# Routed experts of a two-block transformer layer: w3's products with both row halves as one stationary, and seven places for split weight pieces

## The reference, cut to what matters

```python
def first_block(...):
    ...
    ret = head_groupnorm(retention_chunkwise(qh, kh, vh)).reshape(B, S, RET_V_DIM)
    y_a = (ret * jax.nn.silu(z_ret)) @ w_ret_out[l]
    a = u_val * jax.nn.sigmoid(u_gate)
    a = causal_depthwise_conv(a, conv_w[l], conv_b[l])
    a = jax.nn.silu(layernorm(a, conv_ln_g[l], conv_ln_b[l]))
    y_b = (a * jax.nn.silu(z_conv)) @ w_conv_out[l]
    ...
def hierarchical_moe(h, w_router_group, w_router_expert, w1, w3, w2):
    ...
    def run_block(args):
        xblk, e = args
        hid = jax.nn.silu(xblk @ w1[e]) * (xblk @ w3[e])
        return hid @ w2[e]
    ...
```

## Time and profile before

| | |
|---|---|
| median of 3 runs | 1822.02 us |
| profiled execution: its own time | 1816.51 us |
| profiled execution: span from first to last instruction | 1814.7 us |
| mean granted TensorE clock | 0.966 of full |
| busy: TensorE, DVE, ACT, POOL | 93%, 62%, 50%, 47% of the span |
| transfers | 340.94 MB, mean 188 GB/s |

### The profile page before, as it was taken

How to read it: one execution, slowest core, us unless ns; L and a number is a source line. 1 busy time by engine, 2 the same in 40 slices (tenths; PEclk the granted TensorE clock), 3 DMA queues, 4 the chain that set the end, 5 groups by cost and what they waited for, 6 DMA issues and landing times.

```text
span 1814.7 us, 23104 instructions
## 1 busy us (share of the span) xinstructions
PE 1688.7 (93%) x7444; PEld 1240.8 (68%) x7444; DVE 1127.6 (62%) x1455; ACT 914.0 (50%) x1228; POOL 861.7 (47%) x451
## 2 busy tenths in 40 slices
PE   2899999989999999899899997967999999999996
PEld 2788888677878787778656786764565666656654
DVE  5776773562232575435354454256999899998996
ACT  4544542532223332243242234334888888888885
POOL 0688886233434244334002331203766777667774
PEclk9899999999999999999899998988999999999998
DMA  8344353222122062613111511055999999999994
GB/s 301 106 112 122 115 193 104 99 93 99 62 84 93 20 242 98 232 47 135 47 69 71 160 53 41 0 232 203 359 376 371 378 374 373 383 372 390 383 375 149
DMA packets 135406, 340.94 MB, mean 188 GB/s; under 512 B 14581, under 2 KB 66045, under 8 KB 110506
## 3 DMA queue, kind: packets, MB, share of 16 engines
q1 hardware_dynamic: 127938, 320.71, 48.7%
q0 software_dynamic: 5200, 8.41, 2.1%
q10 hardware_dynamic: 2200, 10.92, 1.5%
HBM read 329.78 MB, written 18.87 MB: 192 GB/s over the span
## 4 chain that ended last, share of the span: by engine, by line
PE 65%; POOL 10%; issue 9%; DVE 8%; ACT 4%; DMA 2%; DVEq 1%; POOLq 0%; ACTq 0%; SPq 0%
PE ps L710 16%; PE ps L711 16%; PE ps L712 16%; POOL parts L2363 7%; PE ps L682 5%; PE ps L914 3%; PE ps L1058 3%; PE ps L692 2%; POOL out L2386 2%; PE ps L1059 2%; ACT arena L1481 2%; DVE arena L2254 1%; DMA ring<-in_w_ada 1%; PE ps L903 1%; PE ps L1020 1%
## 5 line engine op out<-in xcount | busy, mean ns | idle before, releaser
L2330 POOL TENSOR_TENSOR parts<-ring,parts 128x1024 fp32r<-128x1024 f32 x158 | 392.2, 2488 | 705.7 <-ACT parts L1108 656.3
L710 PE MATMUL ps<-parts,act_parts 128*128 128x512 f32 (+2 forms) x1152 | 453.6, 394 | 13.7 <-DVEq L1738 5.3
L712 PE MATMUL ps<-parts,act_parts 128*128 128x512 f32 (+2 forms) x1152 | 449.1, 390 | 0.0
L711 PE MATMUL ps<-parts,act_parts 128*128 128x512 f32 (+2 forms) x1152 | 448.6, 389 | 0.0
L1451 ACT CAST parts<-ring 128x1024 fp32r<-128x1024 f32 x384 | 396.4, 1048 | 93.5 <-PE ps L712 70.0
L2214 DVE TENSOR_TENSOR parts<-ring,parts 128x1024 fp32r<-128x1024 f32 x289 | 394.4, 1415 | 25.1 <-ACT parts L1451 18.2
L1108 ACT CAST parts<-ring 128x1024 fp32r<-128x1024 f32 x158 | 163.9, 1048 | 348.7 <-PE ps L712 305.2
L2363 POOL TENSOR_TENSOR parts<-ring,parts 128x1024 fp32r<-128x1024 f32 x95 | 262.3, 2761 | 143.7 <-ACT parts L1451 143.0
L710 PEld LDWEIGHTS ps<-parts,act_parts 128*128 128x128 f32 (+1 forms) x1152 | 190.0, 165 | 105.5 <-POOL parts L2363 18.8
L710 PE MATMUL ps<-act_parts,parts 128*128 128x512 f32 x640 | 252.2, 394 | 5.2 <-DVEq L1641 5.2
L711 PE MATMUL ps<-act_parts,parts 128*128 128x512 f32 x640 | 249.9, 390 | 0.0
(11 more groups left out here) (265 smaller groups left out, 1794.6 us busy)
## 6 DMA issues: line engine op xcount, KB each, us to landing
ring<-in_w SPq DMA_DIRECT2D x192, 1024.0 KB, 7.4
ring<-in_w_in SPq DMA_DIRECT2D x30, 1024.0 KB, 7.3
ring<-in_w_in SPq DMA_DIRECT2D x34, 512.0 KB, 5.2
ring<-in_w_ada SPq DMA_DIRECT2D x12, 1024.0 KB, 15.0
ring<-in_w_ret_out SPq DMA_DIRECT2D x8, 1024.0 KB, 6.2
ring<-in_w_out SPq DMA_DIRECT2D x8, 1024.0 KB, 8.6
ring<-in_w_in SPq DMA_DIRECT2D x16, 256.0 KB, 4.1
gates_dram<-arena ACTq DMA_DIRECT2D x8, 512.0 KB, 5.8
```

Source lines behind the costliest of these rows:

```text
L710: pe.matmul(o, lhs[1], rhs[0], start=start, stop=False)
L711: pe.matmul(o, lhs[0], rhs[1], start=False, stop=False)
L712: return pe.matmul(o, lhs[0], rhs[0], start=False, stop=stop)
L2330: pool.tensor_tensor(parts[:, g % 4, 1, :], ring[:, st.place(j), k * 1024:(k + 1) * 1024], parts[:, g % 4, 0, :].bitcast(F32), ALU.subtrac ...
```

## The change

In the experts:

- The parts get seven places: piece n of a block stands in place n % 7, four of them in `parts` and three in a stretch of `act_parts` that is free at that time. TensorE frees them by two semaphores, `up_used` and `down_used`.
- w3's products take both halves of the rows as one stationary of 128x128, as w2's did: two matmuls for each 128 rows of the weight in place of three. `xgT` is laid out for it.
- The result of w3 then has low rows; ACT copies them (`low_up`, L1481 of the changed kernel, a copy of 64x512) and DVE adds them (`up_sum`, L2273) before `hidden`'s product (L2279), whose operands are then all in SBUF.
- The gate is one step: ACT's Silu of w1's product; DVE's `gate` is gone.

In the first block Silu takes the place of a sigmoid and a product in the same way, for z (L1254, L1745 are gone) and for the convolution (L1230, L1232, L1728 become one Silu).

The diff, cut to its core. The places:

```diff
+        more_parts = act_parts[:, 2048:8192].rearrange("p (s h n) -> p s h n", s=3, h=2)
+        def piece_parts(n):
+            return parts[:, n % 7] if n % 7 < 4 else more_parts[:, n % 7 - 4]
```

TensorE, `up`:

```diff
-                for j in range(2):
-                    o = bank(stage, 1 + j, i)[0:SLOTS, :]
-                    for n in range(4):
-                        pe.wait_ge(piece_split[4 * j + n], b + 1)
-                        for c in range(2):
-                            t = 2 * n + c
-                            mm = split_product(o, hi_lo(xgT[:, :, t, :]), hi_lo(parts[:, n, :, c * 512:(c + 1) * 512]),
...
+                for n in range(8):
+                    if n % 4 == 0:
+                        o = bank(stage, 1 + n // 4, i)
+                    pe.wait_ge(piece_split[n], b + 1)
+                    w = piece_parts(n)
+                    for c in range(2):
+                        t = 2 * (n % 4) + c
+                        half = slice(c * 512, (c + 1) * 512)
+                        if n < 4:
+                            mm = split_product(o[0:SLOTS, :], [xgT[:, t, h, :] for h in range(2)], [w[:, h, half] for h in range(2)],
                                                t == 0, t == KT - 1)
                         else:
+                            rows = xgT[:, t].rearrange("p h s -> p (h s)")
+                            pe.matmul(o, rows, w[:, 0, half], start=t == 0, stop=False)
+                            mm = pe.matmul(o, rows, w[:, 1, half], start=False, stop=t == KT - 1)
```

ACT, in the convolution and in the experts:

```diff
-                    own(act.activation(convT[:, t, :], convT[:, t, :], ACT.Identity, bias=bias, scale=g))
-                    own.wait()
-                    act.activation(ln_s[:, t % 2, :], convT[:, t, :], ACT.Sigmoid).then_inc(ln_s_ready, 1)
+                    act.activation(convT[:, t, :], convT[:, t, :], ACT.Silu, bias=bias, scale=g).then_inc(ln_s_ready, 1)
...
+            def gate(stage, i=0):
+                drained(stage, 1, act.activation(t_h[0:SLOTS, :], full(stage, 1, i)[0:SLOTS, :], ACT.Silu))
+            def low_up(stage, i=0):
+                act.copy(up_low[0:SLOTS, :], full(stage, 2, i)[SLOTS:2 * SLOTS, :]).then_inc(up_low_ready, 1)
...
+            def round(b, i):
+                high(7, b, used=(up_used, b * 6 + 1))
+                gate("moe", i)
+                for n in (8, 9):
+                    high(n, i, used=(up_used, b * 6 + (n - 6)))
+                high(10, i)
+                high(11, i, used=(up_used, b * 6 + 4))
+                low_up("moe", i)
+                high_rows("moe", 0, i)
...
             with act.Fori(0, act.snap(steps - 1)) as r:
-                up("moe", r + 2, 0, r + 1, ends=("moe", 5, r))
+                high(0, r + 2, ends=("moe", 2, r))
+                for n in (1, 2, 3):
+                    high(n, r + 2, used=(down_used, r * 3 + n))
                 low_rows(r)
                 high_hidden("moe", r)
-                up("moe", r + 2, 4, r + 1, ends=("moe", 1, r + 1))
-                down(r + 1)
-                high_rows("moe", 0, r + 1)
+                for n in (4, 5, 6):
+                    high(n, r + 2)
+                round(r + 2, r + 1)
```

DVE, in the convolution and in the experts:

```diff
-                        own(dve.tensor_tensor(convT[:, q, :], convT[:, q, :], ln_s[:, q % 2, :], ALU.mult))
-                        own.wait()
...
+            def hidden(stage, b, i=0):
+                dve.wait_ge(up_low_ready, b + 1)
+                moe(dve.tensor_tensor(up_sum[0:SLOTS, :], full(stage, 2, i)[0:SLOTS, :], up_low[0:SLOTS, :], ALU.add))
                 moe.wait()
+                drained(stage, 2, dve.nop())
...
-                moe(dve.scalar_tensor_tensor(out=hid[0:SLOTS, :], in0=full(stage, 2, i)[0:SLOTS, :], scalar=w,
+                moe(dve.scalar_tensor_tensor(out=hid[0:SLOTS, :], in0=up_sum[0:SLOTS, :], scalar=w,
                                              in1=t_h[0:SLOTS, :], op0=ALU.mult, op1=ALU.mult))
...
                 for n in (4, 5, 6):
                     low(n, r * 12 + (20 + n))
-                gate("moe", r + 2, r + 1)
                 for n in (8, 9, 10):
                     low(n, r * 12 + (20 + n))
```

More of the change, by code:

```diff
@@ L386, in build @@
         y_low = carve([D])
+        up_low, up_sum = carve([FF]), carve([FF])
         block_w = block_oh
@@ L452, in build @@
         piece_used = [sem(f"parts{n}_used") for n in range(4)]
-        moe_used = [sem(f"moe_parts{n}_used") for n in range(3)]
+        up_used, down_used, up_low_ready = sem("up_pieces_used"), sem("down_pieces_used"), sem("up_low_rows_ready")
         dense_split = sem("dense_pieces_split")
@@ L1250, in _ @@
                 for m in range(MT):
-                    o = full(f"hz{h}", m)
-                    if m >= 2:
-                        act.wait_ge(sig_r_used, h * MT + (m - 1))
-                    act.activation(sig_r[:, m % 2, :], o, ACT.Sigmoid).then_inc(sig_r_ready, 1)
+                    own(act.activation(z_tok[:, m, :], full(f"hz{h}", m), ACT.Silu))
+                    own.wait()
+                    drained(f"hz{h}", m, act.nop())
+                    act.nop().then_inc(z_ready, 1)
                 ahead(g + 12)
@@ L1468, in high_rows @@
             def high_rows(stage, k, i=0):
-                act.copy(xgT[:, 0].rearrange("p t n -> p (t n)"), full(stage, k, i)).then_inc(xgT_hi, 1)
-            def up(stage, b, first, i=0, ends=None):
-                for n in range(first, first + 3):
-                    high(n, b, used=pieces[stage].before(n, i))
-                high(first + 3, b, ends=ends)
-                if first == 4:
-                    act.activation(sg_h[0:SLOTS, :], full(stage, 1, i)[0:SLOTS, :], ACT.Sigmoid).then_inc(sg_h_ready, 1)
+                act.copy(xgT[:, :, 0, :], full(stage, k, i).rearrange("p (t n) -> p t n", t=KT)).then_inc(xgT_hi, 1)
+            def gate(stage, i=0):
+                drained(stage, 1, act.activation(t_h[0:SLOTS, :], full(stage, 1, i)[0:SLOTS, :], ACT.Silu))
+            def low_up(stage, i=0):
+                act.copy(up_low[0:SLOTS, :], full(stage, 2, i)[SLOTS:2 * SLOTS, :]).then_inc(up_low_ready, 1)
             def low_rows(c):
@@ L1740, in head_rows @@
             def head_rows(h):
-                for m in range(MT):
-                    o = full(f"hz{h}", m)
-                    dve.wait_ge(sig_r_ready, h * MT + m + 1)
-                    own(dve.tensor_tensor(z_tok[:, m, :], o, sig_r[:, m % 2, :], ALU.mult))
-                    own.wait()
-                    dve.nop().then_inc(sig_r_used, 1)
-                    drained(f"hz{h}", m, dve.nop())
                 dve.wait_ge(decay_in, (h + 1) * 16)
@@ L2292, in _ @@
                 low(n, 8 + n)
-            gate("moe", 1)
             for n in (8, 9, 10):
```

94 lines of the change are left out of this document (42 added, 52 removed).

## The result

| | before | after |
|---|---|---|
| median of 4 runs each | 1821.88 us | 1937.22 us (1934.97 to 1940.58) |
| ratio | | 1.0635, 95% interval 1.0619 to 1.0651 |
| profiled execution: its own time, span | 1816.51, 1814.7 us | 1940.58, 1938.7 us |
| a round, mean of 29 (first to thirtieth scatter) | 17.36 us | 21.68 us |

The change makes the kernel 6.3% slower. The 29 rounds grew by 29 x 4.32 = 125.3 us and the whole span by 124.0 us, so the rest of the program, the first block's gain included, comes out at about zero in these two profiles.

A forecast was written before the change was run, and what follows sets the result against it. With the change, DVE's queue, held up by POOL's lows, was to bound the rounds: 15.06 + 6.60 - 0.4 = 21.3 us. Rounds +118 us and first block -8.5 us gave 1926, forecast as a 1931 us median, range 1840 to 1965 us.

The forecast's parts named there:

- TensorE is not alone at its end: Experts' rounds: w3's fewer matmuls save TensorE 1.8 us a round, worth its price only if TensorE is last.
- A block costs 2.20 us, and there are three in a round: Experts' rounds: three POOL lows each hold up a DVE instruction with two SBUF inputs, 2.20 us each, 6.60 us together.
- The prediction's other price: Experts' rounds: POOL's whole shortest low, 2.34 us, per block instead of 2.20; 0.4 us more a round, some 13 us in all.
- Where they fall: DVE's round: POOL's low 7 blocks low 8, low 11 blocks low 9, low 3 blocks the next round's low 0.
- the sign of two long lows between low 6 and the product: DVE's round: two DVE lows in a row at 3.3 us or more there would show the forecast right.
- Low 11 without a wait for ACT: POOL's round: high 11 is ready, so low 11 follows low 7 at once, taking its turn after DVE's low 8.
- First block, 8.5 us: First block: DVE's chain to the group norm ends 7.1 us earlier; TensorE gains 8.5 us from wait and transposes.
- Transfers have 2 us of room: Experts' rounds: 6.55 MB a round needs 15.4 us at 425 GB/s, so weight transfers do not end last.
- the blocks stay as cheap: Rival: POOL's lows keep meeting DVE's PSUM work, DVE needs 16.8 us a round; 1796 us, chance 0.11.
- one block hidden: Rival: low 3 or low 11 escapes blocking a DVE low; 19.1 us a round, 1865 us, chance 0.12.
- packed without a gap: Rival: mutually exclusive DVE and POOL work runs gapless; 17.7 us a round, 1824 us, chance 0.06.
- TensorE's clock: Rival: TensorE, idle some 3 us a round in one piece, slows; 1.2 us more a round, 1967 us, chance 0.06.

The follow-up runs named there:

- E4: The changed kernel with w3's product as before: three matmuls, no `low_up`, no `up_sum`, product reading PSUM; 1920.39 us, ratio 1.0509, 21.07 us a round.
- E1: The kernel before with only the first block's edits (one Silu for z, one for the convolution), experts unchanged; 1817.71 us, ratio 0.9950.
- E7: The changed kernel reordered: POOL does low 7, scatter, low 11, gather; DVE does low 3; gate's result in PSUM; 2144.61 us, ratio 1.1768.
- E10: As E9, but the gate's result in SBUF, so both inputs of the product are in SBUF; 1843.47 us, ratio 1.0119.
- E12: As E9, but POOL's wait for the scatter's landing moved from its round's end to behind the next gather; 1801.36 us, ratio 0.9872.
- E2: The changed kernel with all twelve lows of a round on DVE and none on POOL; 1837.73 us, ratio 1.0061.
- E3: The changed kernel with POOL's three lows cut to 16 columns of 1024, waits and order kept; 1789.31 us, ratio 0.9792.
- E8: As E7, but the gate's result in SBUF, so both inputs of the product are in SBUF; 2154.06 us, ratio 1.1808.
- E9: As E7, but POOL gathers first and waits for the scatter's landing last; high 7 waits for w1's end; 1829.58 us, ratio 1.0049.

## Why the prediction was right

*TensorE is not alone at its end; its 1.8 us are worth nothing here.* Right. TensorE is busy 79% of the rounds (75% forecast), and E4, with its old work, has shorter rounds than the changed kernel.

*A block costs 2.20 us, and there are three in a round.* Right in number and price: in the 25 rounds DVE's nine lows take 17.1 us a round in the mean, which is three blocks of 2.2 us over the 10.56 us of nine alone. In the round shown the three are 2.56, 2.14 and 2.17 us, and without them it is 21.89 - 6.87 = 15.0 us, as the 15.06 us of the prediction. The sum was 21.3 us, the mean 21.68. The 0.4 us that `rest` was to cover for low 3 was not covered, since low 3 starts 1 us into the next triple; with it the sum is 21.7. The prediction's other price, 2.34 us and 0.4 us more in a round, would have given the same 21.7 us for a reason that the 25 rounds do not bear out.

*Where they fall.* Half right. Low 11 blocks one of 8, 9, 10 and low 3 one of 0, 1, 2, as forecast. Low 7 was to block low 8. It starts at 1407.36, 2.5 us after the end of `add_rows` (0.40 us ahead of 1405.24) and not 3.1, and blocks low 6. The 3.1 us of the earlier trace rows held a wait for high 7 (0.17 us, behind the whole 1.50 us of the scatter's row); with high 7 there, POOL takes low 7 up 1.04 us after the scatter's start, not 1.66. So the sign of two long lows between low 6 and the product did not show: there is one. For the sum it made no difference which low was held.

*Low 11 without a wait for ACT.* Not quite: 0.60 us in the round shown, and up to 3.8 us (46.2 us in 24 waits). High 11 stands behind the gate on ACT, and the gate waits for w1's end (84.7 us in 25 waits), since TensorE is now late. The early release frees high 11 from w3's end, but not from w1's. The prediction also gave DVE a turn between lows 7 and 11 when the one follows the other at once. E4 shows that it gets none (6.12 us for one low); the price of the two, 4.9 us, is still near twice 2.20.

*First block, 8.5 us.* Right by E1: 9 us (6 to 12). The chain became 7.7 us shorter, where the sum had 7.1. The profile of the changed kernel alone would show 4.6 us (371.21 to 366.65). There the chain takes the same 10.5 us as in E1, but begins 3.1 us late (356.15). TensorE had made 89 matmuls in the first 50 us and not 105. In E4 to E7 and E10 to E12 it had made 89 to 92 too, and in E1, E2, E3, E8 and E9 103 to 105, so this goes with no edit of this study, and its cause is open.

*Transfers have 2 us of room.* Not shown, and without effect on this sum. The step took 15.4 us from the 425 GB/s of a stretch of 12 us in the earlier trace rows. The best of E3's stretches of 100 us had 406 GB/s, which is 16.1 us for the 6.55 MB of a round, and E3's later rounds ran at 376 GB/s with ACT waiting. E12's rounds, 17.07 us, are held by the chain shown there and not by transfers.

*The sum.* 1931 us forecast, 1937 measured. The rounds cost 125 us where the sum had 118, and in the two profiles the first block's gain does not show in the whole span. The forecast's growth was 109.5 us; the medians lie 115 us apart and the two profiled spans 124. So it is in part luck that the median comes this near.

The rivals: 'the blocks stay as cheap', 'one block hidden' and 'packed without a gap' are out by the rounds of 21.7 us. TensorE's clock did fall (0.92 in the rounds), but E4 had 0.99 and 21.07 us, and three whole blocks already make 21.7 us, so it is not what made the round.
